# Moving the sine product of a complex scan's state from VectorE to GpSimd

## The reference, cut to what matters

```python
def s5_mixer(h, a_re, a_im, log_dt, b_re, b_im, c_re, c_im, d_skip, w_glu):
    u = h.reshape(B, L, N_GROUPS, SSM_GROUP)          # 64 groups of 16 channels, 64 states each
    dt = exp(log_dt)[:, None]
    decay = exp(a_re * dt)
    ab_re, ab_im = decay * cos(a_im * dt), decay * sin(a_im * dt)
    ...                                               # bb = coef * b (complex)
    bu_re = einsum('blgc,gpc->blgp', u, bb_re)        # the drive
    bu_im = einsum('blgc,gpc->blgp', u, bb_im)
    # x[t] = ab * x[t-1] + bu[t], complex, along the tokens
    x_re, x_im = associative_scan(complex step, (ab, bu))
    y = einsum('blgp,gcp->blgc', x_re, c_re) - einsum('blgp,gcp->blgc', x_im, c_im)
    y = y + d_skip * u
    g = gelu(y)
    ga, gb = split(g @ w_glu)
    return ga * sigmoid(gb)
```

## Time and profile before

| quantity | value |
|---|---|
| median of 3 executions | 1734.09 us (1732.87 to 1734.72) |
| profiled execution, its own time | 1734.25 us |
| profiled execution, span from first to last instruction | 1732.5 us |
| TensorE busy | 1680.5 us (97%) |
| VectorE busy | 780.0 us (45%) |
| ScalarE busy | 312.6 us (18%) |
| GpSimd busy | 58.7 us (3%) |
| mean granted TensorE clock | 0.991 of full |

### The profile page before, as it was taken

The page is one execution under the profiler, slowest core; times in us unless marked ns, Lnnn a source line. Parts: engine busy times, 40 slices in busy tenths (PEclk is TensorE's granted clock), DMA queues, the critical chain, the costliest instruction groups (busy, mean ns, idle before and its releaser), DMA issues.

```text
span 1732.5 us, 23056 instructions
## 1 busy us (share of the span) xinstructions
PE 1680.5 (97%) x9354; PEld 1422.2 (82%) x9354; DVE 780.0 (45%) x1686; ACT 312.6 (18%) x686; POOL 58.7 (3%) x84
## 2 busy tenths in 40 slices
PE   7999999999999999999999999999999898999998
PEld 6758888888888868888888785788888787788887
DVE  6645354323365414654345576466542272433310
ACT  2131210000052102100001323322220121122200
POOL 0000000000000000290000000000000000000000
PEclk9999999999999999999999999999999899999999
DMA  6445468875654664766554232244435303444455
GB/s 221 128 136 172 152 235 306 289 241 190 211 170 160 225 223 140 249 219 224 181 166 147 85 121 97 91 141 153 151 123 170 122 3 101 140 149 157 148 162 177
DMA packets 78297, 289.23 MB, mean 167 GB/s; under 512 B 8688, under 2 KB 8688, under 8 KB 77424
## 3 DMA queue, kind: packets, MB, share of 16 engines
q1 hardware_dynamic: 78192, 287.76, 49.3%
HBM read 286.67 MB, written 1.05 MB: 166 GB/s over the span
## 4 chain that ended last, share of the span: by engine, by line
PE 93%; DVE 5%; issue 1%; ACT 1%; DMA 0%; SPq 0%; DVEq 0%; ACTq 0%
PE acc L380 71%; PE acc L449 5%; PE acc L435 3%; PE acc L944 3%; PE acc L390 1%; PE acc L560 1%; PE score L584 1%; PE score L540 1%; PE score L650 1%; PE score L896 1%; PE acc L611 1%; DMA ring<-stream 0%; PE turned L595 0%; PE acc L871 0%; PE acc L910 0%
## 5 line engine op out<-in xcount | busy, mean ns | idle before, releaser
L380 PE MATMUL acc<-H,ring 128*128 128x256 f32 x3528 | 770.2, 380 | 7.3 <-DVE H L1451 3.0
L380 PEld LDWEIGHTS acc<-H,ring 128*128 128x128 f32 x3528 | 667.0, 190 | 108.7 <-issue 11.5
L380 PE MATMUL acc<-FFN,ring 128*128 128x256 f32 x1408 | 306.5, 381 | 0.0
L380 PEld LDWEIGHTS acc<-FFN,ring 128*128 128x128 f32 x1408 | 268.5, 191 | 37.3 <-issue 0.4
L380 PE MATMUL acc<-big,ring 128*128 128x256 f32 x880 | 192.1, 379 | 0.9 <-PE acc L380 0.9
L380 PEld LDWEIGHTS acc<-big,ring 128*128 128x128 f32 x880 | 166.9, 190 | 24.6 <-issue 2.0
L1608 DVE SCALAR_TENSOR_TENSOR bT<-bT,cond 128x1024 f32<-128x1024 f32 x58 | 75.7, 1305 | 77.8 <-DMA bT<-ada_in 74.1
L1803 DVE SCALAR_TENSOR_TENSOR pair<-acc,cols,pair 128x255 f32<-128x255 f32 x84 | 40.5, 482 | 121.1 <-ACT pair L1121 117.9
L1466 DVE TENSOR_TENSOR X<-acc,X 128x256 f32<-128x256 f32 x48 | 20.4, 425 | 147.7 <-PE acc L380 138.7
L1468 DVE SCALAR_TENSOR_TENSOR X<-acc,mod,X 128x256 f32<-128x256 f32 x24 | 11.6, 484 | 148.4 <-PE acc L380 145.0
L1121 ACT ACTIVATE pair<-acc,cols 128x256 f32<-128x256 f32 x84 | 47.2, 564 | 161.7 <-PE acc L380 161.7
(11 more groups left out here) (411 smaller groups left out, 1366.8 us busy)
## 6 DMA issues: line engine op xcount, KB each, us to landing
ring<-stream SPq DMA_DIRECT2D x440, 512.0 KB, 3.5
bT<-ada_in SPq DMA_DIRECT2D x70, 512.0 KB, 4.5
big<-ada_in SPq DMA_DIRECT2D x26, 512.0 KB, 4.4
big<-ssm_in SPq DMA_DIRECT2D x2, 1024.0 KB, 5.7
cols<-cols_in SPq DMA_DIRECT2D x1, 1169.5 KB, 7.2
X<-x_in SPq DMA_DIRECT2D x1, 1024.0 KB, 4.8
MEM<-mem_in SPq DMA_DIRECT2D x1, 1024.0 KB, 12.2
y_out<-X SPq DMA_DIRECT2D x1, 1024.0 KB, 3.9
```

The costliest lines, as they stand in the source:

```text
L380: mm = nc.tensor.matmul(dst, w[:, k * cols_per:(k + 1) * cols_per], r, start=first and n == 0, stop=last and n == len(src) - 1)
```

## The change

The product of the scanned state with the sine leaves VectorE and becomes one GpSimd instruction per tile. The factor -1 is removed from it: the drive is negated instead, so the scan yields the negated state, and the cosine products carry the signs (the -1 moves from the imaginary to the real one). The scanned state `w`, which was one place in `FFN`, alternates between two places in `SQ`. Two semaphores are new: `s5_scanned` (the scan of tile n has finished; GpSimd and the decays of ScalarE wait for it) and `s5_turned` (the sine product has finished; TensorE's `read_out` and VectorE's scan of the tile after next wait for it).

```diff
@@ TensorE, read_out(n)
                 pe.wait_ge(s5_state, n + 1)
+                pe.wait_ge(s5_turned, n + 1)
                 x = at(FFN, 16 + 4 * ((n + 1) % 2), 4)
@@ ScalarE, decays(n)
                 if n >= 2:
-                    act.wait_ge(s5_state, n - 1)
+                    act.wait_ge(s5_scanned, n - 1)
@@ GpSimd, at the end of its program
             pool.sem_inc(s5_angle, 1)
+            for n in range(KD):
+                i = S5_ORDER[n]
+                w, x = at(SQ, 2 * (n % 2), 2), at(FFN, 18 + 4 * ((n + 1) % 2), 2)
+                sin_i = chunk_tab[:, 2048 + i * S:2048 + (i + 1) * S]
+                if n < 2:
+                    pool.wait_ge(s5_shifted, 4 * n + 4)
+                if n >= 2:
+                    pool.wait_ge(s5_y, n - 1)
+                pool.wait_ge(s5_scanned, n + 1)
+                g.tensor_tensor(x.rearrange("p (k t) -> p k t", t=S), w.rearrange("p (k t) -> p k t", t=S),
+                                sin_i.unsqueeze(1).broadcast_to([P, 2, S]), ALU.mult).then_inc(s5_turned, 1)
@@ VectorE, the loop over the tiles
-                a, b, z, w = (at(FFN, 8 + 2 * e, 2) for e in range(4))
+                a, b, z = (at(FFN, 8 + 2 * e, 2) for e in range(3))
+                w = at(SQ, 2 * (n % 2), 2)
...
-                own(v.tensor_tensor(z[:, re], a[:, re], b[:, im], ALU.add))
-                own(v.tensor_tensor(z[:, im], a[:, im], b[:, re], ALU.subtract))
+                own(v.scalar_tensor_tensor(z[:, re], a[:, re], -1.0, b[:, im], ALU.mult, ALU.subtract))
+                own(v.tensor_tensor(z[:, im], b[:, re], a[:, im], ALU.subtract))
                 dve.wait_ge(s5_decays, n + 1)
+                if n >= 2:
+                    dve.wait_ge(s5_turned, n - 1)
                 own(v.tensor_tensor_scan(w, d, z, 0.0, ALU.mult, ALU.add))
+                dve.sem_inc(s5_scanned, 1)
                 if n < 2:
                     dve.wait_ge(s5_shifted, 4 * n + 4)
                 if n >= 2:
                     dve.wait_ge(s5_y, n - 1)
-                own(v.tensor_tensor(x[:, re], w[:, re], cos_i, ALU.mult))
-                own(v.scalar_tensor_tensor(x[:, im], w[:, im], -1.0, cos_i, ALU.mult, ALU.mult))
-                own(v.scalar_tensor_tensor(by_tile(x[:, 2 * S:4 * S]), by_tile(w), -1.0, sin2, ALU.mult, ALU.mult))
+                own(v.scalar_tensor_tensor(x[:, re], w[:, re], -1.0, cos_i, ALU.mult, ALU.mult))
+                own(v.tensor_tensor(x[:, im], w[:, im], cos_i, ALU.mult))
                 dve.sem_inc(s5_state, 1)
```

More of the change, by code:

```diff
@@ L277, in build_program @@
         s5_gained = sem("s5_gained")
+        s5_scanned = sem("s5_scanned")
+        s5_turned = sem("s5_turned")
         s5_shifted = sem("s5_shifted")
```

## The result

The changed kernel took 1736.1 us (median of 16 executions, 1735.13 to 1739.24) against 1733.86 us for the kernel before (16 executions, 1732.2 to 1734.89). The ratio is 1.0018, with a 95% interval of 1.0011 to 1.0025: 3.1 us slower, and 1.9 to 4.3 us by the interval. That is a loss clear of the noise, just inside the 0.2% that the prediction called no change. The ratio is larger than the difference of the medians (2.2 us) because half of the changed kernel's executions lie at 1735.1 to 1735.8 and the other half is spread from 1736.4 to 1739.2. The profiled execution is one of the low half: 1735.22 us, span 1733.4 us.

A forecast was written before the change was run, and what follows sets the result against it. TensorE makes up 93% of the chain; VectorE counts where `read_out(7)` waits for it. Five tiles at +0.33 us give +1.6 us, clock 0: from the median 1734.09 to 1735.7 us, range 1732.9 to 1738.5 us.

The forecast's parts named there:

- Where VectorE counts: Mixer's tile loop: what tiles 3 to 7 gain or lose on VectorE moves `read_out(7)` and the kernel's end equally.
- The order of the two engines, and the hold: After each scan: first cosine product, then GpSimd holding 1.13 us, then the second product; `s5_state` 0.33 us later per tile.
- T: The end of a tile's scan on VectorE; 1434.14 us for tile 7 in the profile before.
- the first rival: After the scan GpSimd goes ahead of VectorE's first cosine product: +0.53 us a tile, +2.7 us, 1736.8 us; chance 0.22.
- The extra signal: VectorE's added signal `s5_scanned` after each tile's scan: +0.10 us a tile.
- The sum over five tiles: Tiles 3 to 7 each lose 0.33 us on VectorE: +1.6 us at the start of `read_out(7)`.
- The clock, taken as 0: TensorE's low clock from `read_out(7)` on: change in its cost taken as 0, range -0.5 to +1.7 us.
- The wait for `s5_turned` on TensorE, called free: TensorE's second wait ahead of `read_out`: free, since `s5_turned` comes at T + 1.7, before `s5_state`.

The follow-up runs named there:

- e3: Changed kernel with GpSimd's product replaced by a fill with zeros that only writes the same place; one execution, 1731.4 us, no ratio.
- e2: Changed kernel with GpSimd started only after both cosine products (waits for `s5_state`, `s5_scanned` left out); ratio 1.0016 to the kernel before.
- e7: Changed kernel with GpSimd after the cosine products, one TensorE wait per tile, last tile's sine product on VectorE; 1729.46 us, ratio 0.9980 to the kernel before.
- e8: Changed kernel with GpSimd's product issued as two instructions of 128x256; ratio 1.0009 to the kernel before.
- e1: Changed kernel with the sine product kept on VectorE, without GpSimd and `s5_turned`; 1733.61 us, ratio 1.0002 to the kernel before.
- e6: Changed kernel with TensorE waiting for `s5_state` alone; VectorE waits for `s5_turned` before signalling it; 1735.47 us, ratio 1.0012 to the kernel before.
- e4: Changed kernel with unused filler products on TensorE, 3 before `read_out(6)` and 7 before `read_out(7)`; ratio 1.0008 to the kernel before.
- e9: e7 with TensorE's wait for `s5_state` put back ahead of that for `s5_turned`; 1736.77 us, ratio 1.0021 to the kernel before.
- e10: Kernel before with one more TensorE wait ahead of each `read_out`, on a semaphore long past its value; ratio 1.0004 to the kernel before.

## Why the prediction was right, and what it missed

The predicted time was 1735.7 us, the measured one 1736.1; no change was forecast, with a sum of +1.6 us. That the two times lie 0.4 us apart is in part luck: the kernel before stood at 1734.09 us for the prediction and at 1733.86 in the comparison, and by the ratio the loss was 3.1 us (1.9 to 4.3), nearly twice the sum. The mechanism is borne out, and one step is not. By its steps:

- **Where VectorE counts.** Right. TensorE's wait ahead of `read_out(7)` carried what tiles 3 to 7 lost.
- **The order of the two engines, and the hold.** Right: the first cosine product (line 2134) at T + 0.15, GpSimd at T + 0.20, held until T + 1.69 (predicted 1.69), the second product done at T + 1.98 (predicted 1.97). That was read from a handful of rows 650 us ahead of the edit. `e3` shows that it is GpSimd's reads, `e2` and `e7` that products from PSUM do not collide, and `e8` that the ports change hands between instructions. Tile 0 took the other order, the first rival: VectorE idled 0.52 us after the scan, GpSimd started 0.31 us ahead of it in 1.27 us, and VectorE's first product took 1.24 us.
- **The extra signal.** 0.10 us predicted, 0.11 measured in `e1`.
- **The sum over five tiles.** +1.6 predicted; +1.65 between tile 3 and `read_out(7)` in the profile, +1.8 in tiles and +2.1 us in time (0.5 to 3.6) in `e6`.
- **The clock, taken as 0.** Its range of -0.5 to +1.7 holds the +0.85 of the profiled execution. Over many executions no difference is clear: filling helps both kernels about equally.
- **The wait for `s5_turned` on TensorE, called free.** This is the step that does not hold. It is free as a wait, since in the change the signal is early. But with it a stall of 1.1 to 2.3 us appears inside `read_out(3)`: in the one profile each of the change, `e2`, `e4`, `e8` and `e9`, and in none of the seven kernels with one wait. `e9` against `e7` shows its price where TensorE sets the pace, 7 us. In the change's profile VectorE's slower tile covers it: `driven(5)` ends at 1416.78 + 2.00 = 1418.78, and VectorE starts tile 5 at 1419.02, 5.84 us after tile 4. It is argued, not shown, that the rest of the loss (3.1 - 2.1 = 1.0 us, with intervals that also allow nothing) comes from executions where the stall was longer than this cover, as in `e4`. Nor are the executions up to 1739.24 us explained by it, since the kernel before has some above 1738 too.

What stays open is what decides when the block is fetched. Late fetches for `read_out(3)` came only with a second wait and signals that come just ahead of it; `e10` and `e3` have a second wait with earlier signals, and no such stall. One reading, e9's theory, fits: in `e9` the transfer starts 1.1 us after GpSimd's product ends (1409.24 + 1.27), so after both waits are met, and in `e7` 1.0 us before that (1413.77 + 1.27), so ahead of the only wait. No run here moves the fetch by itself, so this is not shown.

## What to carry to other kernels

Moving work to GpSimd beside VectorE gained nothing where both read SBUF at that moment: 0.73 us taken off VectorE came back as 0.95 us of waiting and 0.11 us for a signal. Started where VectorE works from PSUM, with one wait on TensorE and the last tile left on VectorE, the same move gained 3.5 us (`e7`). Look for "issue" stalls inside streams of small products, and count such a stream also by its instructions: here 128 products took 2 us, and it paid to let TensorE wait once, for the signal that implies the other.

## What the runs showed of the hardware that was not expected

- An additional wait, for a signal that the next wait implies, cost TensorE 7 us (1729.46 to 1736.77 us): in the profile a stall of 2.27 us in which no engine is waited for, and a low clock of 6.8 us behind it.
- Every profile has such a stall of 1.56 to 2.44 us near 1290 us in a stretch of small products, whatever the edit. Behind the stalls of `read_out(3)` the products went on 2.4 to 2.9 us after the start of an instruction transfer, and in the kernel before, near 1290 us, 2.3 us after it.
- A GpSimd fill of 128x512 (0.53 us) does not disturb VectorE's products with two SBUF inputs at all; a product of the same shape (1.27 us) stops them for 0.95 us.
- A start 0.05 us earlier was enough for VectorE to go first with its instruction (0.42 us), and the gap of 0.04 us before its next one was enough for GpSimd to come in between.
